# Attention output built transposed, with normalised probabilities, in a two-layer decoder trunk

## The chip, the cores and the metric

One core of a Trainium2 chip, which has eight in two dies. The metric is the device time of one execution in microseconds (us), given as the median of several runs. Everything is float32.

## What is computed

Two layers of a hybrid decoder trunk over 512 tokens of width 1024. Each layer normalises, projects, runs attention (8 query heads that share 2 key heads, 3 branches) beside a gated convolution, projects out, and then runs a channel mixer: dense in the first layer, the two best of 8 experts in the second.

```python
h = rms_norm(x, norm1[layer])
proj = h @ w_in[layer]          # q, 3 x (k, v), gates, conv B, C, h
...
s = einsum(q, k) * scale + rel_bias      # per branch, causal
p = masked_softmax(s, mask)              # exp(s - max) / sum
o = gc[..., 0:1] * o_cmp + gc[..., 1:2] * o_slc + gc[..., 2:3] * o_win
...
mixed = concatenate([rms_norm(o_attn, attn_out_norm[layer]),
                     rms_norm(o_conv, conv_out_norm[layer])], axis=-1)
x = x + mixed @ w_out[layer]
h = rms_norm(x, norm2[layer])
x = x + swiglu(h, ...)          # or moe_swiglu in the second layer
```

With 512 tokens the best 16 of 8 blocks are all blocks and the window covers everything, so the selected and the sliding branch (b = 0 and 1) are both plain causal attention with their own keys and values. The compressed branch attends to 31 blocks.

## The kernel before

The kernel is written in Bass: each engine has its own program, in an order written out by hand, and waits on semaphores. TensorE (pe), VectorE (dve), ScalarE (se), GpSimd (pool) and the DMA queue (sp) run beside each other. Both layers call the same function `layer(L)`.

A layer has these parts. The norm and its turns to hT. The projections of q (four tiles of 128 tokens), k and v, compressed k and v and gates (`natural`, `channels`, L795 and L801), with the turns of queries and keys (L817, L824). The compression (L868, L876). Then the attention loop, of NP + 2 = 34 steps. At its end the sums of the convolution's squares (L985) and the projection out (L1007), whose results VectorE adds to x.

**The attention loop.** Step p has query tile t = p // 8, q = p % 8, the branch b = p % 2 and one pair of heads; a unit u is one head of it (two in a step), over n = 128 (t + 1) keys. For each unit:

- `scores` (L898, TensorE): 64 rows of qT against 64 rows of kT, n columns, into bank u % 2. The two heads of a step lie in the two halves of the rows.
- `scores` (L1199, VectorE): adds the bias from T, negates, keeps the row's extreme. Writes sb_s.
- `probs` (L1421, ScalarE): exponential into sb_p, with the row's sum in `den`.
- `turn` (L911, TensorE): t + 1 transposes of 128 x 128 into bank 2, one step later.
- `pt_copy` (L1207 on VectorE for even units, L1429 on ScalarE for odd ones): bank 2 to sb_pt.
- `values` (L920, TensorE): t + 1 products, turned probabilities stationary (128 columns), values moving (64 columns), into columns of bank 4 (b = 0) or 5 (b = 1).

Between these TensorE's `fill` (L855) gives out products of the convolution's projections, one of 8 for each third of a channel tile, with 512 columns in bank 3. `STEP_FILL` says how many go into each of the three places of a step. When a third is full, ScalarE copies it (`conv_c`, L1386) or VectorE reads it (`conv_z`, L1135, or `conv_b`, L1148); the next third waits for that. `conv_taps` (L1142 to L1144) and `conv_sum` (L1158) are VectorE's too.

Once in a tile come the compressed branch: `cmp_scores` (L932; VectorE L1216 to L1219), `cmp_probs` (L1438), `cmp_turn` (L939), `cmp_values` (L945, into bank 7); and then `coefs` (L1230 to L1232: one over the sums, times the gates), `combine` (L1245 to L1250: the three banks, each times its coefficient, added up in `on`), `attn_norm` (L1448: the sum of squares), `gain` (L1254), `o_turn` (L951: four transposes to bank 7) and `o_copy` (L1452) to mixT, which the projection out reads. For the last tile the turn stands between the projection's first and second token tile.

The functions that the change touches, and the loops that call them:

## Time and profile before

| | us |
|---|---|
| median of 3 runs | 2334.39 (2327.37 to 2335.43) |
| profiled execution | 2332.5 |
| its span in the profile | 2330.7 |
| TensorE busy | 2216.8 (95%) |
| VectorE busy | 397.0 (17%) |
| ScalarE busy | 277.4 (12%) |

The profile is of one execution. Products in float32 leave two records each, transposes one. A record's own duration is longer than its share of the engine, since records overlap in the pipeline; the distance from one start to the next tells what a piece costs. The timeline merges neighbouring records of one line into a piece. Most of the 2330 us are products of the feed-forward and of the experts; the two attention loops take about 170 us each.

### The profile page before, as it was taken

How to read it: one execution, taken by the hardware profiler on the slowest of the kernel's cores; microseconds unless marked ns; L12 is line 12 of the kernel's file. 1: busy time of each engine (PE TensorE's matmuls, PEld its weight loads, DVE VectorE, ACT ScalarE, POOL GpSimd, SP SyncE). 2: the span in 40 equal slices, each digit the busy share in tenths (PEclk: the TensorE clock that was granted, in tenths of full speed). 3: DMA queues.
4: the chain of work that ended last, by engine and by line, in shares of the span. 5: the costliest groups of instructions: out<-in, count | busy, mean ns of one | idle time of the engine just before them, and what ended most of it. 6: DMA issues, size and time to landing. Idle time of an engine off the chain costs nothing.

```text
span 2330.7 us, 29764 instructions
## 1 busy us (share of the span) xinstructions
PE 2216.8 (95%) x12796; PEld 1665.9 (71%) x12796; DVE 397.0 (17%) x1080; ACT 277.4 (12%) x752; POOL 70.3 (3%) x79
## 2 busy tenths in 40 slices
PE   7999998999999989999966999999999999999994
PEld 3556644444444445566556999999999999999994
DVE  2235422000000022254231001010000101010102
ACT  1133311000000012233100000000000000000000
POOL 1100000000000011000000000000000000000001
PEclk9999998999999989999967999999999999999997
DMA  8101106222210402000018556767777777878743
GB/s 322 56 37 37 37 9 266 77 72 72 83 62 0 200 9 72 37 37 1 1 50 356 218 221 244 282 257 287 272 281 276 277 290 283 308 289 304 289 181 118
DMA packets 43987, 382.83 MB, mean 164 GB/s; under 512 B 5362, under 2 KB 5394, under 8 KB 14544
## 3 DMA queue, kind: packets, MB, share of 16 engines
q1 hardware_dynamic: 36208, 355.68, 41.0%
q0 software_dynamic: 4768, 14.92, 2.0%
q10 hardware_dynamic: 2880, 10.32, 1.1%
q8 instruction: 102, 1.67, 0.3%
q14 instruction: 29, 0.24, 0.0%
HBM read 368.46 MB, written 14.54 MB: 164 GB/s over the span
## 4 chain that ended last, share of the span: by engine, by line
PE 93%; DVE 3%; DMA 1%; issue 1%; ACT 1%; POOL 1%; POOLq 0%; DVEq 0%; ACTq 0%
PE ps L382 29%; PE ps L391 14%; PE ps L1022 13%; PE ps L855 7%; PE ps L1031 6%; PE ps L795 6%; PE ps L1007 5%; PE ps L920 2%; PE ps L911 2%; PE ps L898 2%; PE ps L801 1%; PE ps L868 1%; DVE work L1079 1%; PE ps L363 1%; PE ps L339 1%
## 5 line engine op out<-in xcount | busy, mean ns | idle before, releaser
L382 PE MATMUL ps<-work,arena 128*128 128x136 f32 (+3 forms) x5632 | 704.8, 284 | 0.7 <-issue 0.7
L382 PEld LDWEIGHTS ps<-work,arena 128*128 128x128 f32 x5632 | 686.9, 192 | 1.2 <-issue 0.8
L391 PE MATMUL ps<-hid,arena 128*128 128x136 f32 (+3 forms) x2816 | 364.7, 283 | 0.0
L391 PEld LDWEIGHTS ps<-hid,arena 128*128 128x128 f32 x2816 | 348.4, 191 | 0.1
L1022 PE MATMUL ps<-hT,arena 128*128 128x512 f32 x704 | 304.6, 596 | 0.8 <-issue 0.8
L1022 PEld LDWEIGHTS ps<-hT,arena 128*128 128x128 f32 x704 | 134.8, 192 | 170.1 <-issue 170.1
L552 DVE TENSOR_TENSOR hid<-sg,ps 128x136 f32<-128x136 f32 (+3 forms) x176 | 52.8, 300 | 900.2 <-ACT sg L653 899.6
L855 PE MATMUL ps<-hT,arena 128*128 128x512 f32 x384 | 197.6, 617 | 2.0 <-ACT gc L1386 2.0
L653 ACT ACTIVATE sg<-ps 128x136 f32<-128x136 f32 (+3 forms) x176 | 50.5, 287 | 928.4 <-PE ps L382 928.4
L1031 PE MATMUL ps<-arena 128*128 128x512 f32 x352 | 151.3, 593 | 0.8 <-DVE arena L1310 0.8
L795 PE MATMUL ps<-arena,hT 128*128 128x512 f32 (+1 forms) x384 | 131.9, 503 | 0.0
L920 PEld LDWEIGHTS ps<-arena,work 128*128 128x128 f32 x640 | 90.7, 193 | 52.4 <-issue 52.4
L1031 PEld LDWEIGHTS ps<-arena 128*128 128x128 f32 x352 | 67.0, 190 | 85.2 <-issue 83.5
L1007 PE MATMUL ps<-arena 128*128 128x512 f32 x256 | 110.8, 594 | 1.5 <-ACT arena L1452 1.5
L795 PEld LDWEIGHTS ps<-arena,hT 128*128 128x128 f32 x384 | 67.3, 207 | 59.0 <-issue 59.0
L855 PEld LDWEIGHTS ps<-hT,arena 128*128 128x128 f32 x384 | 63.5, 197 | 41.6 <-issue 37.4
L1007 PEld LDWEIGHTS ps<-arena 128*128 128x128 f32 x256 | 48.4, 190 | 61.1 <-issue 61.1
L1421 ACT ACTIVATE work<-work,st 128x128 f32<-128x128 f32 (+3 forms) x128 | 71.8, 561 | 160.3 <-PE ps L911 107.8
L920 PE MATMUL ps<-arena,work 128*128 128x64 f32 x640 | 85.7, 266 | 0.0
L1199 DVE CUSTOM_DVE_ANT_0 work<-ps,arena 128x128 f32<-128x128 f32 (+3 forms) x128 | 57.9, 488 | 111.4 <-PE ps L898 103.5
L1515 POOL TENSOR_TENSOR st<-st,cst 128x1 f32<-128x1 f32 (+3 forms) x38 | 40.5, 1066 | 1125.8 <-DVE st L1058 1125.7
L911 PEld LDWEIGHTS ps<-cst,work 128*128 128x128 f32 x320 | 38.5, 149 | 42.1 <-issue 28.4
(201 smaller groups left out, 991.1 us busy)
## 6 DMA issues: line engine op xcount, KB each, us to landing
arena<-m_w SPq DMA_DIRECT2D x176, 1536.0 KB, 6.6
arena<-f_gu SPq DMA_DIRECT2D x22, 1024.0 KB, 5.0
arena<-w_cv SPq DMA_DIRECT2D x8, 1536.0 KB, 21.6
arena<-f_dn SPq DMA_DIRECT2D x11, 1024.0 KB, 4.8
arena<-w_o SPq DMA_DIRECT2D x4, 2048.0 KB, 7.5
arena<-w_q SPq DMA_DIRECT2D x2, 2048.0 KB, 12.0
arena<-w_kv SPq DMA_DIRECT2D x2, 2048.0 KB, 16.3
arena<-bias_by_query_and_key SPq DMA_DIRECT2D x2, 2048.0 KB, 8.8
```

The source lines that it names most:

```text
L382: m = mm(ps[:, s % 2, j * CAP:j * CAP + W], w[:, k, :], xT[:, k, 0:W], start=(k == 0), stop=(k == KD - 1))
L391: m = mm(ps[:, 2 + j // 2, (j % 2) * CAP:(j % 2) * CAP + W], down_w[s % NSLOT][:, j * P:(j + 1) * P], hid[:, s % 2, 0:W], start=(s == 0 an ...
L552: v.tensor_tensor(hid[:, s % 2, 0:W], sg[:, s % 2, 0:W], ps[:, s % 2, CAP:CAP + W], ALU.mult).then_inc(hid_done, 1)
L795: m = mm(ps[:, bank, col:col + n], hT[:, k, t * P:(t + 1) * P], w[:, k, :], start=(k == 0), stop=(k == KD - 1))
L855: m = mm(ps[:, 3, :], cv_w[CO[i]][:, k, j * P:(j + 1) * P], hT[:, k, :], start=(k == 0), stop=(k == KD - 1))
L911: m = tr(ps[:, 2, i * P:(i + 1) * P], sb_p[:, u % 2, i * P:(i + 1) * P], ident)
L920: m = mm(ps[:, 4 + b, h * DH:(h + 1) * DH], sb_pt[:, u % 2, i * P:(i + 1) * P], V[:, i, b * P + (h // R) * DH:b * P + (h // R + 1) * DH], ...
L1007: m = mm(ps[:, b0 + j, :], mixT[:, 4 * part + k, t * P:(t + 1) * P], WO[part][:, k, hf * 512:(hf + 1) * 512], start=(k == 0), stop=(k == 3))
L1022: m = mm(ps[:, 2 * (i % 2) + j, :], w[:, k, :], hT[:, k, :], start=(k == 0), stop=(k == KD - 1))
L1031: m = mm(ps[:, 2 * t + hf, :], down_w[s][:, i * 512 + t * P:i * 512 + (t + 1) * P], slot[s][:, i * D + hf * 512:i * D + (hf + 1) * 512], s ...
L1199: v.tensor_tensor_reduce(sb_s[:, u % 2, 0:n], ps[:, u % 2, 0:n], T[:, h, 384 - P * t:384 - P * t + n], -1.0, 3e38, ALU.add, ALU.min, negm[ ...
L1421: act(sb_p[:, u % 2, 0:n], sb_s[:, u % 2, 0:n], ACT.Exp, bias=negm[:, u % 16:u % 16 + 1], scale=-1.0, accum_out=den[t % 2][:, 1 + b, h:h + ...
```

## The change

The output of the attention is built with channels on partitions.

- `values`: the values are stationary (64 columns) and the turned probabilities move (128 columns). Key group 0 writes partitions 0 to 63, group 1 partitions 64 to 127 of one bank, 4 + t % 2, into which all three branches of a tile add up. Heads are paired across the groups (r and r + 4), so each step has one head of each group. A step's values run two steps after its scores, in one piece; sb_pt has a second pair of buffers.
- `scale` (new, VectorE): as the sum over branches is now made in the bank, each probability is multiplied by its gate over its sum ahead of the turn, in place. `turn` waits for `scaled`, not for `p_done`. For the compressed branch `cmp_scale` does that.
- `cmp_values`: eight products with 64 stationary columns, added into the tile's bank, in step q = 0 of the next tile.
- `coefs`, `combine`, `gain`, `attn_norm`, `o_turn` and `o_copy` go. New are `o_squares` (ScalarE, from the bank), `evacuate` (VectorE, bank times gain to mixT), `o_reduce` (VectorE, sum over the four column groups) and `o_total` (TensorE, sum over partitions, one column). The sums of the convolution's squares (`conv_totals`) and of the last tile move between the products of the projection's first token tile; one reciprocal root serves all eight sums.
- Keys are no longer doubled for two row halves: kT has 2 groups instead of 4, and the key turns, the key gains and the compressed keys are half as many.
- `STEP_FILL` has the same number of products in another order; `cmp_scores` moves from q = 5 to q = 4.
- Weights for q and w_out are laid out by head pairs on the host.

The diff, cut to its core:

```diff
-STEP_FILL = ((1, 1, 1), (1, 1, 1), (1, 1, 0)) + 2 * ((0, 1, 1), (1, 1, 1), (1, 1, 1)) + (
-    (0, 1, 3), (1, 1, 1), (0, 1, 0), (0, 1, 1), (1, 1, 1), (1, 1, 1), (0, 1, 1), (0, 1, 1), (0, 1, 3),
-    (0, 1, 1), (1, 1, 1), (1, 1, 1), (0, 1, 1), (1, 1, 1), (1, 1, 1), (0, 1, 1), (0, 1, 3), (1, 0, 1),
-    (0, 1, 1), (1, 1, 1), (1, 1, 1))
+STEP_FILL = ((1, 1, 1), (1, 1, 1), (1, 1, 0)) + 9 * ((0, 1, 1), (1, 1, 1), (1, 1, 1))
...
-        sb_s, sb_p, sb_pt = w2[:, 0], w2[:, 1], w2[:, 2]
+        sb_s, sb_p = w2[:, 0], w2[:, 1]
+        sb_pt = [w2[:, 2], arena[:, A_KC + 2 * S:A_KC + 4 * S].rearrange("p (b n) -> p b n", b=2)]
...
+                def scores(p):
+                    t, r, b = p // 8, (p % 8) // 2, p % 2
+                    n = P * (t + 1)
+                    if p == 0:
+                        pe.wait_ge(z_done, 2 * L + 2)
+                    else:
+                        pe.wait_ge(sb_done, NU * L + 2 * p)
...
+                        mm(ps[:, g, 0:n], qT[g * DH:(g + 1) * DH, r, t * P:(t + 1) * P], kT[g * DH:(g + 1) * DH, b, 0:n],
+                           start=True, stop=True).then_inc(s_ps, 1)
...
-                    pe.wait_ge(p_done, NU * L + u + 1)
+                    pe.wait_ge(scaled, NU * L + u + 1)
...
-                def values(u):
-                    t, h, b = unit(u)
-                    pe.wait_ge(pta if u % 2 else ptd, NP * L + u // 2 + 1)
-                    if u % 16 == 0 and t:
-                        pe.wait_ge(o_read, TT * L + t)
+                def values(p):
+                    t, r, b = p // 8, (p % 8) // 2, p % 2
+                    pe.wait_ge(ptd, NP * L + p + 1)
+                    pe.wait_ge(pta, NP * L + p + 1)
+                    if p % 8 == 0 and t >= 2:
+                        pe.wait_ge(mix_done, TT * L + t - 1)
+                        pe.wait_ge(osq_done, TT * L + t - 1)
                     for i in range(t + 1):
-                        m = mm(ps[:, 4 + b, h * DH:(h + 1) * DH], sb_pt[:, u % 2, i * P:(i + 1) * P],
-                               V[:, i, b * P + (h // R) * DH:b * P + (h // R + 1) * DH], start=(i == 0), stop=(i == t))
+                        for g in range(G):
+                            m = mm(ps[g * DH:(g + 1) * DH, 4 + t % 2, r * P:(r + 1) * P], V[:, i, b * P + g * DH:b * P + (g + 1) * DH],
+                                   sb_pt[p % 2][:, g, i * P:(i + 1) * P], start=(p % 8 == 0 and i == 0), stop=(b == 1 and i == t and r == R - 1),
+                                   skip_group_check=True)
...
                 def cmp_values(t):
                     pe.wait_ge(cpt_done, TT * L + t + 1)
-                    for g in range(G):
-                        m = mm(ps[:, 7, g * 256:(g + 1) * 256], PcT[:, g, :], vbd[:, g, :], start=True, stop=True)
+                    for r in range(R):
+                        for g in range(G):
+                            m = mm(ps[g * DH:(g + 1) * DH, 4 + t % 2, r * P:(r + 1) * P], vbd[:, g, r * DH:(r + 1) * DH], PcT[:, g, :],
+                                   start=False, stop=False, skip_group_check=True)
                     m.then_inc(co_ps, 1)
 
-                def o_turn(t):
-                    pe.wait_ge(og_done, TT * L + t + 1)
-                    for i in range(4):
-                        m = tr(ps[:, 7, i * P:(i + 1) * P], on[:, i * P:(i + 1) * P], ident)
-                    m.then_inc(ot_ps, 1)
+                def o_total(t):
+                    pe.wait_ge(osum_done, TT * L + t + 1)
+                    mm(ps[:, 7, 448 + t:449 + t], o_sum, ones[:, 0:1], start=True, stop=True).then_inc(sums_ps, 1)
+
+                def conv_totals():
+                    pe.wait_ge(sqs_done, CT * (L + 1))
+                    for t in range(TT):
+                        m = mm(ps[:, 7, 452 + t:453 + t], sqsum[:, t * P:(t + 1) * P], ones[:, 0:1], start=True, stop=True)
+                    m.then_inc(sums_ps, 1)
...
                     if 1 <= p <= NP:
                         turn(2 * p - 2)
                     fill(f[1])
                     if p >= 2:
-                        values(2 * p - 3)
+                        values(p - 2)
+                    if q == 0 and t:
+                        cmp_values(t - 1)
                     if 1 <= p <= NP:
                         turn(2 * p - 1)
                     fill(f[2])
-                    if 1 <= p <= NP:
-                        values(2 * p - 2)
                     if p == 3:
                         cmp_keys()
-                    if q == 4 and t:
-                        o_turn(t - 1)
-                    if q == 5:
+                    if q == 3 and t:
+                        o_total(t - 1)
+                    if q == 4:
                         cmp_scores(t)
                     if q == 6:
                         cmp_turn(t)
-                    if q == 7:
-                        cmp_values(t)
-
-                pe.wait_ge(sqs_done, CT * (L + 1))
-                pe.wait_ge(cpt_done, TT * (L + 1))
-                for t in range(TT):
-                    m = mm(ps[:, 6, t:t + 1], sqsum[:, t * P:(t + 1) * P], ones[:, 0:1], start=True, stop=True)
...
+                        if t == 0 and j == 1:
+                            o_total(TT - 1)
+                            conv_totals()
...
+                def scale(p):
+                    t, r, b = p // 8, (p % 8) // 2, p % 2
+                    n = P * (t + 1)
+                    d = den[:, (2 * p) % 16:(2 * p) % 16 + 2]
+                    dve.wait_ge(p_done, NU * L + 2 * p + 2)
+                    after(v.reciprocal(d, d))
+                    if p == 0:
+                        dve.wait_ge(gate_done, L + 1)
+                    for g in range(G):
+                        v.tensor_scalar(sb_p[:, g, 0:n], sb_p[:, g, 0:n], d[:, g:g + 1], gts[:, t, R * g + r, 1 + b:2 + b],
+                                        ALU.mult, ALU.mult).then_inc(scaled, 1)
+
...
+                def cmp_scale(t):
                     n = KD * t + 7
                     dve.wait_ge(cp_done, TT * L + t + 1)
-                    after(v.tensor_reduce(den[t % 2][:, 0, :], Pc[:, :, 0:n], AX, ALU.add))
-
-                def coefs(t):
-                    dve.wait_ge(p_done, NU * L + 16 * t + 16)
-                    dve.wait_ge(gate_done, L + 1)
-                    dflat = st[:, 40 + 64 * (t % 2):64 + 64 * (t % 2)]
-                    after(v.tensor_scalar(dflat, dflat, 1e-30, None, ALU.max))
-                    after(v.reciprocal(dflat, dflat))
-                    after(v.tensor_tensor(coef, den[t % 2], gts[:, t, :, :].rearrange("p h b -> p b h"), ALU.mult))
+                    after(v.tensor_reduce(denc, Pc[:, :, 0:n], AX, ALU.add))
+                    after(v.tensor_scalar(denc, denc, 1e-30, None, ALU.max))
+                    after(v.reciprocal(denc, denc))
+                    after(v.tensor_tensor(coefc, denc, gts[:, t, :, 0], ALU.mult))
                     if t == 0:
-                        after(v.tensor_scalar(coef[:, 0, :], coef[:, 0, :], cst[:, C_VALID:C_VALID + 1], None, ALU.mult))
-
-                def combine(t):
-                    o3 = on[:, :].rearrange("p (h n) -> p h n", h=H)
-                    t3 = on_t[:, :].rearrange("p (h n) -> p h n", h=H)
-                    bank = lambda b: ps[:, b, :].rearrange("p (h n) -> p h n", h=H)
-                    dve.wait_ge(co_ps, TT * L + t + 1)
-                    if TT * L + t:
-                        dve.wait_ge(ot_ps, TT * L + t)
-                    dve.wait_ge(kct_ps, L + 1)
-                    dve.wait_ge(o_ps, NU * L + 16 * t + 16)
-                    after(v.tensor_tensor(o3, bank(4), bc_last(coef[:, 1, :], DH), ALU.mult))
-                    v.tensor_tensor(t3, bank(5), bc_last(coef[:, 2, :], DH), ALU.mult).then_inc(o_read, 1)
-                    dve.wait_ge(o_read, TT * L + t + 1)
-                    after(v.tensor_tensor(o3, o3, t3, ALU.add))
-                    after(v.tensor_tensor(t3, bank(7), bc_last(coef[:, 0, :], DH), ALU.mult))
-                    v.tensor_tensor(o3, o3, t3, ALU.add).then_inc(comb_done, 1)
-
-                def gain(t):
-                    dve.wait_ge(ssa_done, TT * L + t + 1)
-                    v.tensor_tensor(on[:, :], on[:, :], pb[:, B_AN:B_QN], ALU.mult).then_inc(og_done, 1)
+                        after(v.tensor_scalar(coefc, coefc, cst[:, C_VALID:C_VALID + 1], None, ALU.mult))
+                    v.tensor_tensor(Pc[:, :, 0:n], Pc[:, :, 0:n], bc_last(coefc, n), ALU.mult).then_inc(cps_done, 1)
+
+                def evacuate(t):
+                    dve.wait_ge(osq_done, TT * L + t + 1)
+                    v.tensor_tensor(mixT[:, 0:R, t * P:(t + 1) * P], ps[:, 4 + t % 2, :].rearrange("p (r n) -> p r n", r=R),
+                                    bc_last(pc[:, PC_AN:PC_AN + R], P), ALU.mult).then_inc(mix_done, 1)
+
+                def o_reduce(t):
+                    dve.wait_ge(osq_done, TT * L + t + 1)
+                    if t:
+                        dve.wait_ge(sums_ps, (TT + 1) * L + t)
+                    v.tensor_reduce(o_sum, o_sq.rearrange("p (r n) -> p n r", r=R), AX, ALU.add).then_inc(osum_done, 1)
...
                         pt_copy(2 * p - 2)
+                    if p < NP:
+                        scale(p)
                     if p == 0:
                         cmp_keys()
                     if p == 1:
                         cmp_vals()
-                    if q == 0 and t:
-                        coefs(t - 1)
                     if q == 1 and t:
-                        combine(t - 1)
-                    if q == 3 and t:
-                        gain(t - 1)
+                        evacuate(t - 1)
+                    if q == 2 and t:
+                        o_reduce(t - 1)
+                    if q == 4:
+                        cmp_scores(t)
...
+                def o_squares(t):
+                    se.wait_ge(o_ps, NP * L + 8 * t + 8)
+                    se.wait_ge(co_ps, TT * L + t + 1)
+                    if t:
+                        se.wait_ge(osum_done, TT * L + t)
+                    act(o_sq, ps[:, 4 + t % 2, :], ACT.Square).then_inc(osq_done, 1)
...
-                    if q == 2 and t:
-                        attn_norm(t - 1)
                     if p == 3:
                         cmp_keys()
-                    if q == 4 and t:
-                        o_copy(t - 1)
-                    if q == 5:
+                    if q == 1 and t:
+                        o_squares(t - 1)
+                    if q == 4:
                         cmp_probs(t)
                     if q == 6:
                         cmp_pt(t)
...
```

## Rows read from the trace of the kernel before

**Rows 1.** Busy time in the second layer's attention stage: span, then PE, PEld, DVE, ACT, POOL.

```profile
955.00:1122.00 167.00, 162.06 (x887) 102.36 (x885) 80.65 (x245) 65.66 (x191) 0.69 (x1) 1.00 0.04 13
```

**Rows 2.** Waits of TensorE in the second layer's attention stage: total us, times, longest us.

```profile
PE ps L911 <- DVE work L1207: 3.0, 3, 1.7
PE ps L855 <- ACT gc L1386: 1.0, 1, 1.0
```

**Rows 3.** TensorE's timeline, steps 28 and 29: start us, us, engine line op tiles xrecords.

```profile
1091.13 1.00 PE L920 MATMUL ps<-arena,work 128*128 128x64 f32 x8
1092.06 1.13 PE L898 MATMUL ps<-arena 64*128 64x512 f32 x4
1093.12 1.13 PE L855 MATMUL ps<-hT,arena 128*128 128x512 f32 x2
1094.08 0.60 PE L911 MATMUL ps<-cst,work 128*128 128x128 f32 x4
1094.52 1.02 PE L855 MATMUL ps<-hT,arena 128*128 128x512 f32 x2
1095.38 1.00 PE L920 MATMUL ps<-arena,work 128*128 128x64 f32 x8
1096.22 0.60 PE L911 MATMUL ps<-cst,work 128*128 128x128 f32 x4
...
1098.36 0.61 PE L951 MATMUL ps<-cst,qk 128*128 128x128 f32 x4
1098.90 1.13 PE L898 MATMUL ps<-arena 64*128 64x512 f32 x4
```

**Rows 4.** TensorE's timeline, compression output and first scores, second layer.

```profile
955.51 0.63 PE L876 MATMUL ps<-pc,hidc 128*31 128x64 f32 x8
956.08 0.49 PE L898 MATMUL ps<-arena 64*128 64x128 f32 x4
```

**Rows 5.** TensorE's timeline, end of the loop and projection, second layer.

```profile
1106.20 1.11 PE L898 MATMUL ps<-arena 64*128 64x512 f32 x4
...
1110.45 0.63 PE L911 MATMUL ps<-cst,work 128*128 128x128 f32 x4 [1.72 <-DVE work L1207]
...
1121.34 1.00 PE L985 MATMUL ps<-cst,arena 128*128 128x1 f32 x8
1122.20 13.98 PE L1007 MATMUL ps<-arena 128*128 128x512 f32 x32
1136.02 0.60 PE L951 MATMUL ps<-cst,qk 128*128 128x128 f32 x4
1137.39 1.96 PE L1007 MATMUL ps<-arena 128*128 128x512 f32 x4 [0.77 <-ACT arena L1452]
```

**Rows 6.** Timelines of VectorE and TensorE at the last two key tiles, second layer.

```profile
930.67 0.76 DVE L1122 TENSOR_TENSOR qk<-work,pb 128x256 f32<-128x256 f32 x2
...
931.49 1.12 PE L824 MATMUL ps<-cst,qk 128*128 128x128 f32 x4 [1.37 <-DVE qk L1122]
```

**Rows 7.** Groups of VectorE, second layer's stage: shapes xcount, busy us, mean ns, idle.

```profile
L1199 DVE CUSTOM_DVE_ANT_0 work<-ps,arena 128x512 f32<-128x512 f32 x16 | 10.4, 688 | 18.6 <-PE ps L898 15.8 <-issue 2.7
...
L1199 DVE CUSTOM_DVE_ANT_0 work<-ps,arena 128x256 f32<-128x256 f32 x16 | 6.1, 422 | 12.4 <-PE ps L898 12.3
L1207 DVE COPY work<-ps 128x512 f32<-128x512 f32 x8 | 5.5, 689 | 2.9 <-PE ps L911 2.8
...
L1144 DVE SCALAR_TENSOR_TENSOR arena<-zc,pc,arena 128x512 f32<-128x512 f32 x4 | 3.0, 752 | 0.1
...
L1142 DVE TENSOR_SCALAR arena<-zc,pc 128x512 f32<-128x512 f32 x4 | 1.9, 481 | 0.0
...
L1231 DVE RECIPROCAL st<-st 128x24 f32<-128x24 f32 x4 | 1.2, 303 | 0.1
```

**Rows 8.** Groups of ScalarE, second layer's stage.

```profile
L1421 ACT ACTIVATE work<-work,st 128x512 f32<-128x512 f32 x16 | 11.5, 722 | 26.2 <-PE ps L911 19.0 <-DVE st L1199 7.2
...
L1429 ACT COPY work<-ps 128x512 f32<-128x512 f32 x8 | 4.5, 566 | 2.4 <-PE ps L911 2.4
```

More of the change, by code:

```diff
@@ L89 @@
 A_WC = 2 * SLOT
-assert A_END <= ARENA and 2 * LP * HID <= KD * 512 and CO[2:] == (0, 1) and KCW * KD >= 2 * S
+assert A_END <= ARENA and 2 * LP * HID <= KD * 512 and CO[2:] == (0, 1) and KCW * KD >= 4 * S
 C_ID, C_ONE, C_TRI, C_IOTA = 0, P, 2 * P, 3 * P
@@ L190, in build @@
         rh = st[:, 16:24]
-        ssa = st[:, 24:28]
-        ra = st[:, 28:32]
-        rc = st[:, 32:36]
+        rac = st[:, 24:32]
         posb = st[:, 36:38]
-        den = [st[:, 40 + 64 * i:64 + 64 * i].rearrange("p (b h) -> p b h", b=3) for i in range(2)]
-        coef = st[:, 64:88].rearrange("p (b h) -> p b h", b=3)
+        den = st[:, 40:56]
+        denc = st[:, 56:64]
+        coefc = st[:, 64:72]
         negm = st[:, 88:104]
@@ L822, in kt @@
                     pe.wait_ge(v_done, TT * L + t + 1)
-                    for i in range(4):
+                    for i in range(2):
                         m = tr(ps[:, 4 + t, i * P:(i + 1) * P], kn[:, i * P:(i + 1) * P], ident)
@@ L957, in layer @@
                     if p < NP:
-                        scores(2 * p)
-                        scores(2 * p + 1)
+                        scores(p)
                     fill(f[0])
@@ L1365, in kt @@
                     se.wait_ge(kt_ps, TT * L + t + 1)
-                    nc.scalar.copy(kT[:, :, t * P:(t + 1) * P], ps[:, 4 + t, :].rearrange("p (k n) -> p k n", k=4)).then_inc(kt_done, 1)
+                    nc.scalar.copy(kT[:, :, t * P:(t + 1) * P], ps[:, 4 + t, 0:2 * P].rearrange("p (k n) -> p k n", k=2)).then_inc(kt_done, 1)
                 for a in range(2):
@@ L1407, in cmp_keys @@
                     se.wait_ge(kct_ps, L + 1)
[L1408 removed]
+                    nc.scalar.copy(kcT[:, 0:NCMP], ps[:, 7, 256:256 + NCMP]).then_inc(kct_done, 1)
                 def probs(u):
[L1411 to L1413 removed]
+                    n = P * (u // 16 + 1)
                     se.wait_ge(sb_done, NU * L + u + 1)
```

164 lines of the change are left out of this document (65 added, 99 removed).

## The prediction

> **What bounds the kernel now.** I read the busy time of the attention stage of the second layer first, then who waits for whom, then the order of TensorE's pieces. In that stage of 167 us TensorE is busy for 162, at its full clock; VectorE is busy for 81 and ScalarE for 66 [rows 1]. The list of waits says the same: about 5 us in which TensorE stands still, of which 3.0 are for VectorE's copy of turned probabilities and 1.0 for a ScalarE copy of a convolution third [rows 2]. So an edit is worth what it takes from TensorE's own pieces, until VectorE or ScalarE comes late. The first layer repeats the stage, so what follows is worked out for one layer and doubled. I name a head pair with one branch a step (32 of them, 8 for each query tile t = 0 to 3), and T1 the moment at which TensorE begins the second turn of a step.
>
> **Values on TensorE.** Pieces are told by the distance of their starts. A values group of 8 records (4 key tiles) takes 0.84 us, a turn of four tiles 0.44, a fill product of 512 columns 0.86 [rows 3]: 0.11 us for each record with 128 stationary columns, however few move, which is the weight load, and 0.43 for each with 512 moving columns. After the change a values record has 64 stationary columns and 128 moving ones, and the moving side then sets 0.107 to 0.111 (the turns move 128 columns in that). That the load of half the columns is below this is bounded by L876: its 8 records of 31 columns with 64 moving take 0.57 from start to next start [rows 4]. So the stream is no shorter for one product; it is halved only if the two column halves run side by side. No row shows column halves. Row halves are the nearest: the two score products of 512 columns take 1.06 together, where one full product takes 0.86 [rows 3]. I take side by side.
>
> Such a group has a price of its own, and the scores show it. Before them the values piece is 0.93 instead of 0.84; they take 1.06 where their columns explain 0.85; the fill product behind them takes 0.96 instead of 0.86 [rows 3]. That is 0.40 for going into another split of the array and back. With a load half as long on the way in I take 0.35 (ends: 0, if columns switch freely, and 0.40). A step's values cost 0.22 x 2(t+1) - 0.11 now and 0.22(t+1) + 0.35 then. The difference is +0.23, +0.01, -0.21 and -0.43 us for t = 0 to 3, eight times each: **-3.2 us** in a layer.
>
> On the page TensorEngine Tiling the Trainium skill says (Key Properties) that a change of tiling mode drains TensorE; this trace agrees for row halves, by the 0.40. The same section says that different tiles can load and multiply in parallel; whether that holds for column halves no row here shows. By the first rule alone this term would be +14.6 us in a layer (8 x 0.22 x 10 more), by both it is the -3.2.
>
> **Other work taken from TensorE or given to it.** The output turn goes (0.54 each, three in the loop), and a one-column sum comes for each tile (two records, 0.22): **-1.0**. Compressed values change from 4 records of 256 columns to 8 pairs of 128 and stay at about 0.9, without a switch of their own, since they stand behind values. At the end the convolution sums (0.86) leave the gap ahead of the projection, and the last output turn with its wait (1137.39 - 1136.02 = 1.37) leaves its middle, where ten one-column records (1.08) come in [rows 5]: **-1.15**. The squares, the output's copy and the reduction that these need take 0.6 + 0.7 + 0.7 behind the last values and are hidden by the 6.9 us of the first eight projection products. The key turns are two instead of four, and one VectorE multiply of some 0.4 goes from the chain that ends the 1.37 us wait for the last key tile [rows 6]: **-1.3**, between -0.9 (the turns alone) and -1.8.
>
> **The wait that is added.** Now a turn starts when ScalarE's exponential is ready. Then VectorE must first take both exponentials of the step, a reciprocal of two columns and two multiplies in place. No row shows these; the nearest are L1231 (0.30 for 24 columns) for the first, taken at 0.17 and 0.035 to the next instruction (0.1 to 0.3), and L1142 (0.48 for 512 columns, a new one after 0.41) for each multiply (0.41 to 0.75, the latter with L1144 as the price of its second scalar) [rows 7]. By these prices, shortened for fewer columns, 64 multiplies and 32 reciprocals are some 28 us more VectorE work in a layer; the combination with its gain and coefficients takes about 18 away, evacuation, sums and compressed scaling bring 9. Worse is the order. VectorE now stands blocked in each step until the second exponential is done, and everything that is queued behind it comes later: convolution z, b, taps and sums, compressed scores, and the next step's score reads, for which TensorE's next turn waits.
>
> For t = 3: the second exponential starts at T1 + 0.76 (end of the turn) and takes 0.72 and 0.09 more for its accumulator [rows 8], so VectorE starts at T1 + 1.62, its first scaled half is there at 2.34 and it is free at 2.64. TensorE needs that half at T1 + 0.54 + 0.86 + 0.09 + 1.06 = 2.56 in steps without a first fill, so the plain step just fits, at 5.0 or 5.9 us. But anything of length E that VectorE does then delays its score reads and its copy by E, against a slack of 0.4 us where the next step has no first fill and 1.3 where it has one; and the next convolution third, at T1 + 3.05, waits for z or b, at T1 + 3.37. With z and b at 0.69 (as L1207), taps at 0.48 + 0.75 + 0.75 plus gaps = 2.05 [rows 7] this gives, step by step: t = 3, z with the sum of squares 0.95, taps 0.7. For t = 2 (rows between those shown): z with evacuation 1.1, taps with the sum 1.2, b behind compressed scores 0.9. For t = 1, with 0.42 for a score read [rows 7]: z 0.55, taps with evacuation 1.35, b 0.55, the other three 0.7. For t = 0: 1.2 for compressed keys, b and compressed scaling. In all **+9.3 us** (4 if the slack is twice what I take, 14 at the dearer multiply). Against that the waits of before in these steps go, 1.0 for the ScalarE copy (compressed probabilities no longer stand in front of it), 0.6 for exponentials and 0.6 of VectorE's 3.0 [rows 2]: **-2.2**.
>
> **The last four steps**, which have no fill, are now a chain: turn, exponential, reciprocal, two multiplies, two score reads, copy, turn. Followed from the start of step 30, with VectorE late by compressed scaling (five small passes, put at 0.2 to 0.4 each by L1231 and L1199's short form, 1.5) and b (0.7): the turn of u59 comes at 5.2, step 31 at 6.1, the turn of u60 at 7.5, of u61 at 9.75, of u62 at 12.05, of u63 at 14.55; ScalarE's copy of that (0.57, behind 0.72) ends at 15.9, the last values at 16.9. Before, it was 1122.20 - 1106.20 = 16.0, with a wait of 1.72 in it [rows 5]. The 1.0 more comes on top of 0.86 and of 3 x 0.43 that I credited above: **+3.1**.
>
> **Sum**: -3.2 - 1.0 - 1.15 - 1.3 + 9.3 - 2.2 + 3.1 = +3.55 us in a layer, +7.1 in both. Projection, feed-forward and experts are untouched. The profiled execution took 2332.5 us (span 2330.7), which gives 2339.6; the median of the three runs lies 1.9 above it, so the forecast is **2341.5 us**. The core's own range is 2331 to 2352.
>
> **Rivals.** *The halves run one after the other* (ends slower). Then values cost 0.22(t+1) more in each step, 8 x 0.22 x 10 = 17.8 us in a layer, of which some 4 come back since VectorE's chain gains that time: +17 in a layer, 2368. It decides if a pair of values records takes 0.21 instead of 0.11. For it: no row shows such a pair. Against: row halves do run together. *VectorE's queue stays hidden.* If the steps' slack takes in z, b and taps, the 9.3 go and the last steps remain: -5.75 in a layer, 2323; and a little below if the last steps are shorter. For it: VectorE is idle for half the stage [rows 1]. Against: it is idle in waits, with its work behind them. *The multiplies cost more than L1142*, by their second scalar or since they write what they read: at 0.75 instead of 0.48 for 512 columns the plain step of t = 3 no longer fits by 0.1 to 0.6 us and each listed wait grows: +5 to +8 in a layer more, 2355. *The change isn't what it says*: should the turns still find a scaled half late by a fixed wait, it is the same case.
>
> **How the numbers follow.** Chances: forecast 0.50, halves in turn 0.15, queue hidden 0.20, dearer multiplies 0.15. A measurement of this kernel can tell about 0.5% (11.7 us) from no change: 2322.7 to 2346.1. Faster by more: half of the hidden case and little else, 0.13. Slower by more: the serial and the dear case and a quarter of the forecast's own range, 0.40. The rest, 0.47, is within. The range reaches from 2319 to 2368: it leaves out some of the hidden case and the upper half of the serial one.
>
> **What would show it.** In the profile after: values records in pairs, a group for t = 3 some 1.1 us to the next turn and 0.5 for t = 0 (2.0 would be the serial case); the piece ahead of it lengthened by 0.1; the in-place multiplies at 0.48 us for 512 columns and some 0.3 for 128; TensorE's waits in the stage from 5 us to some 15, on VectorE's scaling, copies and z; VectorE busy for about 100 us of it. The weakest step is the sum of the waits, the next is that column halves pair as row halves do.

## The result, and the profile after

The changed kernel takes 2343.91 us (median of 8 runs, 2340.35 to 2346.39) beside 2331.78 for the kernel before (8 runs, 2327.37 to 2335.86): ratio 1.0048, 95% interval 1.0036 to 1.0059. It is slower by 12.1 us, where 7.1 was forecast. The forecast time of 2341.5 came closer than this, 2.4 us away, because it was counted from the median of three runs of the kernel before, 2334.4, which lies 2.6 above the median of eight; that part of the closeness is luck. The profiled execution took 2343.9, its span 2342.0, against 2332.5 and 2330.7.

The page of the kernel after, span and busy time by engine:

```profile
span 2342.0 us, 30066 instructions
PE 2207.9 (94%) x12858; PEld 1616.3 (69%) x12858; DVE 432.5 (18%) x1236; ACT 270.4 (12%) x736; POOL 69.7 (3%) x77
```

TensorE has 8.9 us less to do than before (2216.8) and the kernel takes 11.3 us more of span: work was traded for waiting. The same second-layer stage as in [rows 1], span, then PE, PEld, DVE, ACT, POOL, and its granted TensorE clock (1.00 is 2.4 GHz, 0.50 is 1.2):

```profile
959.00:1134.00 175.00, 158.00 (x921) 78.18 (x919) 102.35 (x331) 63.70 (x185) 0.69 (x1) 0.98 0.04 13
```

The stage is 175 us instead of 167, TensorE is busy for 158 of it instead of 162, and VectorE for 102 instead of 81. TensorE's waits there, to be set against the 5 us of [rows 2] (total us, times, longest):

```profile
PE ps L906 <- DVE arena L1212: 5.9, 6, 2.6
PE ps L906 <- DVE work L1212: 3.5, 3, 1.8
PE ps L855 <- DVE zc L1130: 2.7, 3, 1.2
PE ps L906 <- DVE work L1204: 2.5, 2, 1.7
PE ps L855 <- DVE arena L1143: 1.7, 3, 0.8
PE ps L918 <- ACT arena L1416: 0.8, 1, 0.8
```

17.1 us. L906 is the turn, L1212 VectorE's copy of turned probabilities, L1204 the new multiply, L855 the fill product, L1130 and L1143 the reads of the convolution's z and b. Only 2.5 us are waits for the multiply itself. The others are for work that VectorE used to have done long before. Why it is late stands in VectorE's groups by shape (shapes, count | busy us, mean ns | idle before, and what ended it):

```profile
L1204 DVE TENSOR_SCALAR work<-work,st,gts 128x512 f32<-128x512 f32 x16 | 8.0, 543 | 0.3
L1204 DVE TENSOR_SCALAR work<-work,st,gts 128x384 f32<-128x384 f32 x16 | 7.0, 477 | 0.3
L1204 DVE TENSOR_SCALAR work<-work,st,gts 128x256 f32<-128x256 f32 x16 | 5.9, 409 | 0.3
L1200 DVE RECIPROCAL st<-st 128x2 f32<-128x2 f32 x32 | 5.3, 166 | 60.2 <-ACT work L1408 60.2
L1204 DVE TENSOR_SCALAR work<-work,st,gts 128x128 f32<-128x128 f32 x16 | 4.8, 344 | 0.3
L1247 DVE TENSOR_REDUCE qk<-qk 128x128 f32<-128x512 f32 x3 | 3.1, 1030 | 0.0
```

The reciprocal's line is the case in one row: VectorE stands for 60.2 us of the stage at the reciprocal, for ScalarE's exponential (L1408), with everything else queued behind it.

The timeline of TensorE in steps 28, 29 (as [rows 3]) and from step 30 to the projection (as [rows 5]):

```profile
1092.41 1.02 PE L855 MATMUL ps<-hT,arena 128*128 128x512 f32 x2
1093.36 1.09 PE L918 MATMUL ps<-work,arena 128*64 128x128 f32 x16
1094.38 0.66 PE L906 MATMUL ps<-cst,work 128*128 128x128 f32 x4
1094.88 1.02 PE L855 MATMUL ps<-hT,arena 128*128 128x512 f32 x2
...
1107.72 0.63 PE L906 MATMUL ps<-cst,work 128*128 128x128 f32 x4 [0.80 <-DVE arena L1212]
...
1115.92 1.13 PE L893 MATMUL ps<-arena 64*128 64x512 f32 x4
...
1121.26 1.09 PE L906 MATMUL ps<-cst,work 128*128 128x128 f32 x4 [2.60 <-DVE arena L1212]
1122.14 0.63 PE L938 MATMUL ps<-cst,Pc 128*128 128x128 f32 x2
1122.71 2.04 PE L893 MATMUL ps<-arena 64*128 64x512 f32 x4
...
1126.84 0.63 PE L906 MATMUL ps<-cst,work 128*128 128x128 f32 x4 [0.48 <-DVE work L1212]
1129.21 0.66 PE L906 MATMUL ps<-cst,work 128*128 128x128 f32 x4 [1.75 <-DVE work L1204]
...
1133.12 1.09 PE L918 MATMUL ps<-arena 128*64 128x128 f32 x16 [0.77 <-ACT arena L1416]
1134.14 2.41 PE L1001 MATMUL ps<-arena 128*128 128x512 f32 x5
```

A values group (L918) of eight pairs of records takes 1.02 us to the next start (1093.36 to 1094.38), the fill product ahead of it 0.95 instead of 0.86 and the turn behind it 0.50 instead of 0.44. Behind the wait of 2.60 the score products take 1.97 us (1122.71 to 1124.68) where two steps earlier they take 1.06 (1115.92 to 1116.98): there TensorE has fallen to half its clock. What it does just before the fall is to stand in that wait.

### The profile page after: what moved, and what is told of

Its sections match the earlier page's. It is cut to its first block, busy times and chain, and to the rows that moved or that the text cites. A ratio compares the mean times of both kernels' runs of the same rounds, so it can differ in the third digit from the quotient of the medians.

```text
span 2342.0 us, 30066 instructions
## 1 busy us (share of the span) xinstructions
PE 2207.9 (94%) x12858; PEld 1616.3 (69%) x12858; DVE 432.5 (18%) x1236; ACT 270.4 (12%) x736; POOL 69.7 (3%) x77
## 4 chain that ended last, share of the span: by engine, by line
PE 90%; DVE 5%; issue 2%; DMA 1%; ACT 1%; POOL 1%; POOLq 0%; DVEq 0%; ACTq 0%
PE ps L382 29%; PE ps L391 14%; PE ps L1019 13%; PE ps L1028 6%; PE ps L855 6%; PE ps L795 6%; PE ps L1001 5%; PE ps L906 2%; PE ps L918 2%; PE ps L893 1%; PE ps L801 1%; PE ps L868 1%; DVE work L1076 1%; DVE work L1204 1%; PE ps L363 1%
## 5 line engine op out<-in xcount | busy, mean ns | idle before, releaser
L1019 PE MATMUL ps<-hT,arena 128*128 128x512 f32 x704 | 304.7, 596 | 0.8 <-issue 0.8
L855 PE MATMUL ps<-hT,arena 128*128 128x512 f32 x384 | 203.6, 629 | 8.6 <-DVE zc L1130 5.3
L855 PEld LDWEIGHTS ps<-hT,arena 128*128 128x128 f32 x384 | 63.4, 198 | 51.2 <-issue 37.6
L1408 ACT ACTIVATE work<-work,st 128x128 f32<-128x128 f32 (+3 forms) x128 | 71.8, 561 | 191.9 <-PE ps L906 110.1
L906 PEld LDWEIGHTS ps<-cst,work 128*128 128x128 f32 x320 | 37.7, 144 | 67.5 <-issue 46.3
L906 PE MATMUL ps<-cst,work 128*128 128x128 f32 x320 | 62.2, 294 | 23.4 <-DVE arena L1212 11.8
L1497 POOL TENSOR_TENSOR st<-st,cst 128x8 f32<-128x8 f32 (+2 forms) x36 | 39.8, 1107 | 1138.0 <-DVE st L1055 1138.0
L1301 DVE TENSOR_TENSOR arena<-work,ps 128x512 f32<-128x512 f32 x22 | 15.2, 689 | 289.3 <-PE ps L1019 289.3
```

Source lines behind the costliest of these rows:

```text
L855: m = mm(ps[:, 3, :], cv_w[CO[i]][:, k, j * P:(j + 1) * P], hT[:, k, :], start=(k == 0), stop=(k == KD - 1))
L906: m = tr(ps[:, 2, i * P:(i + 1) * P], sb_p[:, u % 2, i * P:(i + 1) * P], ident)
L1019: m = mm(ps[:, 2 * (i % 2) + j, :], w[:, k, :], hT[:, k, :], start=(k == 0), stop=(k == KD - 1))
L1408: act(sb_p[:, u % 2, 0:n], sb_s[:, u % 2, 0:n], ACT.Exp, bias=negm[:, u % 16:u % 16 + 1], scale=-1.0, accum_out=den[:, u % 16:u % 16 + 1]) ...
```

## The experiments

All times are medians beside the kernel before on the same chip, which ran at 2332 to 2334 us throughout. Edits are against the changed kernel, unless something else is said.

### Is it the multiply, or where it waits? The scaling taken out

```diff
-                    pe.wait_ge(scaled, NU * L + u + 1)
+                    pe.wait_ge(p_done, NU * L + u + 1)
...
-                    if p < NP:
-                        scale(p)
```

> The changed kernel without its in-place scaling of the two full branches: reciprocal and multiplies are left out (so these two branches are neither normalised nor gated), and a turn waits for the exponential alone, as in the kernel before. Theory (VectorE's queue stands blocked behind the exponentials, and TensorE waits for it): of some 17 us of TensorE's waits in a loop about 13 go, and with them the two stretches at half clock; 15 us in a layer, 2313 us. Rival (the column halves and their switches are dearer than thought, the waits are a minor part): no more than 5 us in a layer, 2334 us.

Measured: 2312.89 us, ratio 0.9919 (0.9898 to 0.994). That is 31 us below the changed kernel; TensorE's waits fall from 33.8 us in both loops to 13.2.

The same work was then left in VectorE's program at the same place and with the same instructions, but on columns that nobody needs, with nothing waited for (the turn waits for the exponential alone, as above):

```diff
-                    d = den[:, (2 * p) % 16:(2 * p) % 16 + 2]
-                    dve.wait_ge(p_done, NU * L + 2 * p + 2)
+                    d = st[:, 200:202]
...
-                        v.tensor_scalar(sb_p[:, g, 0:n], sb_p[:, g, 0:n], d[:, g:g + 1], ...
+                        v.tensor_scalar(spare_p[:, g, 0:n], spare_p[:, g, 0:n], d[:, g:g + 1], ...
```

> The same reciprocals and multiplies in the same places of VectorE's order and of the same sizes, but on spare columns, so that they wait for no exponential and no turn waits for them (the two full branches are neither normalised nor gated). Theory (the wait and the order behind it): nearly as short as without scaling, 2313 to 2322 us. Rival (VectorE has too much work, 102 us instead of 81 in a loop): as the changed kernel, 2338 to 2344 us.

Measured: 2312.28 us, 0.9909 (0.9888 to 0.993), and waits of 14.0 us. The multiplies and reciprocals, 31 us of VectorE in a layer (8.0 + 7.0 + 5.9 + 4.8 + 5.3), cost nothing at all; the 31 us of both layers are the price of the waits around them, VectorE's for the exponentials and the turn's for the scaled probabilities. It also gives a size for what the change takes from TensorE: with these waits away it is some 20 us shorter than the kernel before, though such a kernel neither normalises nor gates.

### Do column halves run side by side?

Both key groups were written to the same column half, so that two products of a pair can't run together:

```diff
-                            m = mm(ps[g * DH:(g + 1) * DH, 4 + t % 2, r * P:(r + 1) * P], ...
+                            m = mm(ps[0:DH, 4 + t % 2, r * P:(r + 1) * P], ...
```

> All products of values and of compressed values write partitions 0 to 63 (the second group's output goes on top of the first's, so the attention output is wrong): both products of a pair are in the same column half. Theory (halves run side by side in the changed kernel): a values group of t = 3 goes from 1.02 to some 1.87 us, 16 to 18 us in a layer less some 4 of waits, 2368 to 2378 us. Rival (the halves ran in turn anyway): 2344 us.

Measured: 2373.89 us (one run), 30 above the changed kernel. The values group of that kernel:

```profile
1117.64 1.96 PE L918 MATMUL ps<-work,arena 128*64 128x128 f32 x16
1119.53 0.66 PE L906 MATMUL ps<-cst,work 128*128 128x128 f32 x4
```

1.89 us for the same sixteen records against 1.02. Over a layer that is 0.87/4 x 8 x 10 = 17.4, and 3.7 more for the compressed values (1.84 instead of some 0.9, four times); twice that is 42, of which 6.9 come back since the waits fall from 33.8 to 26.9. The 5 us that are left may be the clock, with 6.8 us at half clock in the loops of this profile against 20.5. Side by side is what the changed kernel has.

### Is it VectorE's order? The work of once a tile ahead of the scaling

Evacuation, compressed keys and convolution taps now stand in front of `scale(p)` in VectorE's step, where it has nothing to do but wait; the evacuation moves to q = 2 and compressed keys and values one step on:

```diff
                         pt_copy(2 * p - 2)
-                    if p < NP:
-                        scale(p)
-                    if p == 0:
-                        cmp_keys()
                     if p == 1:
+                        cmp_keys()
+                    if p == 2:
                         cmp_vals()
...
                         conv_taps(i)
+                    if p < NP:
+                        scale(p)
+                    if p == NP + 1:
+                        evacuate(TT - 1)
+                    if q == 4:
+                        cmp_scores(t)
```

> Only VectorE's order is changed: convolution taps and sums, the compressed scaling, evacuation (one step later) and reduction stand ahead of the step's scaling, in the time in which VectorE waited for the exponentials; compressed keys and values one step later. Nothing is left out. Theory: of the waits on copies (1.24, 0.36, 0.44, 1.31, 0.38, 1.76, 0.80 and 2.60 in the second layer) about 6 us go in a layer, those on z and b (4.3) stay; 2330 to 2334 us. Rival (total of VectorE's work decides): 2342 to 2346 us.

Measured: 2322.81 us, 0.995 (0.9933 to 0.9967). Of the 31 us that the waits cost, 21 are the order of the queue behind them, much more than I expected. Its waits in the second layer's stage:

```profile
PE ps L906 <- DVE work L1204: 3.5, 4, 1.7
PE ps L855 <- DVE arena L1143: 1.7, 3, 0.8
PE ps L906 <- DVE arena L1212: 1.2, 1, 1.2
PE ps L855 <- DVE zc L1130: 1.1, 3, 0.5
PE ps L918 <- ACT arena L1417: 0.8, 1, 0.8
PE ps L906 <- DVE work L1212: 0.7, 1, 0.7
```

The waits for copies went from 9.4 to 1.9 and those for z from 2.7 to 1.1; the one for the multiply itself, 3.5, is now the largest.

### Can the convolution's thirds wait instead?

```diff
-STEP_FILL = ((1, 1, 1), (1, 1, 1), (1, 1, 0)) + 9 * ((0, 1, 1), (1, 1, 1), (1, 1, 1))
+STEP_FILL = ((1, 1, 1), (1, 1, 1), (1, 1, 0)) + 9 * ((0, 0, 2), (1, 1, 1), (1, 1, 1))
```

> The changed kernel with (0, 0, 2) instead of (0, 1, 1) in the nine steps that begin a convolution third: the third's first product stands behind the second turn instead of ahead of the values. Theory: TensorE's waits on z and b (0.52, 0.46, 0.34, 0.97, 0.79, 1.23: 4.3 us in the second layer) go, but the values and the second turn come 0.86 earlier and meet VectorE's copy, which gives a part of it back in the steps behind evacuation or taps; 2336 to 2341 us. Rival (the wait only moves to the copy): 2343 to 2346 us.

Measured: 2350.27 us, 1.0069 (1.0046 to 1.0093). The expectation was wrong in sign, with four runs from 2343.6 to 2352.8. The waits for z and b are gone, as meant, and the waits for copies take their place and more:

```profile
PE ps L906 <- DVE arena L1212: 7.9, 7, 2.6
PE ps L906 <- DVE work L1212: 7.3, 6, 2.1
PE ps L906 <- DVE work L1204: 2.5, 2, 1.7
PE ps L918 <- ACT arena L1416: 0.8, 1, 0.8
```

The product that was taken from between the turn and the values had been the cover of VectorE's late copy. With VectorE as late as here, holding a product back didn't mend the wait: it moved it to the next place where the two meet.

### What the fill order is worth

In the kernel before, with the changed kernel's `STEP_FILL` and nothing else:

> The kernel before with nothing changed but the order of the convolution's products among the steps, which is that of the changed kernel. The new order has no part in the loss if this is as before, 2330 to 2335 us; if it has one, the thirds that end in steps with compressed work meet ScalarE and VectorE there and cost up to 5 us in a layer, 2342 us. The theory says the first, with at most 2 us in a layer.

Measured: 2341.47 us, 1.0034 (1.0022 to 1.0045), some 8 us where at most 4 were expected. Its waits in the second layer:

```profile
PE ps L908 <- DVE work L1204: 3.6, 3, 1.7
PE ps L917 <- DVE qk L1243: 1.4, 3, 0.5
PE ps L852 <- ACT gc L1383: 1.0, 1, 1.0
PE ps L852 <- DVE zc L1132: 0.5, 1, 0.5
```

L917 is that kernel's values and L1243 its read of a bank in `combine`. The old order gave three products to the place behind the second turn in steps 9, 17 and 25, where `combine` stands. These waits explain 5 of the 8 us (15.8 in both loops, 10.8 before). Its profile also has 13.7 us of its loops at half clock against 6.8, which by the sizes found below is 1.5 to 3 us more. What is left I can't name by a row.

And the other way round, the changed kernel with the old order:

> The change with the fill order of the kernel before, and nothing else altered. In the kernel before, the changed kernel's fill order alone cost 7 to 9 us, because it takes away the three products that stand beside VectorE's combine. Here combine is gone. Theory A (the old order was fitted to combine, so it is worth nothing without it): within 3 us of the changed kernel, 2341 to 2347, or slower, up to 2350, because it holds three products back for places where nothing waits. Theory B (the old order is better whatever VectorE does): 2334 to 2339, the whole difference to the kernel before given back.

Measured: 2343.1 us, 1.0047 (1.003 to 1.0064), as the changed kernel itself. Theory A holds: an order fitted to `combine` is worth 8 us with it and nothing without it. So the new order isn't a part of the loss.

### What the clock costs: products in the longest wait

Two more products of 512 columns in each layer, whose result nobody reads, where TensorE waits 2.60 us:

```diff
+                    if p == NP - 2:
+                        pe.wait_ge(cv_done, CT * (L + 1))
+                        for k in range(2):
+                            mm(ps[:, 3, :], hT[:, k, 0:P], hT[:, k, :], start=True, stop=True)
```

> The changed kernel with two more products of 512 columns (results unused, 1.7 us of work) in step 30 of each layer, in the 2.6 us in which TensorE waits for a copy. Theory (the wait lowers the granted clock, and the pieces behind it then run at 1.2 GHz): no stretch at half clock behind step 30 and 1 to 3 us in a layer less in spite of the added work; 2338 to 2342 us. Rival (the clock falls for another reason): the fall stays, 2344 us or a little above.

Measured: 2342.71 us, 1.0043 (1.0026 to 1.006), with more work in it no slower than the changed kernel; the 1.2 us between them are within the noise. The same 8 us of both kernels, the clock is the figure ahead of the last two (the changed kernel first, then this one):

```profile
1117.00:1125.00 8.00, 5.40 (x35) 3.23 (x34) 5.37 (x16) 3.37 (x8) 0.00 (x0) 0.79 0.00 1
```

```profile
1117.00:1125.00 8.00, 6.40 (x50) 3.54 (x46) 6.14 (x18) 4.32 (x10) 0.00 (x0) 1.00 0.00 1
```

In this profile the fall behind this wait is gone in both layers; one early in each loop is left. This makes it likely that the wait brings the fall and doesn't show it, since a wait of the same length can stay without one. Here are such a wait in the first layer of the changed kernel with the old fill order, and the 8 us around it, with the clock at 1.00:

```profile
295.18 0.63 PE L909 MATMUL ps<-cst,work 128*128 128x128 f32 x4 [2.60 <-DVE arena L1215]
```

```profile
291.00:299.00 8.00, 4.93 (x50) 3.38 (x50) 6.11 (x18) 3.91 (x9) 0.00 (x0) 1.00 0.66 258
```

In three profiles with this wait (changed, old fill order, thirds later), each with two layers, four of the six waits have a fall beside their end and two have none. With the two products in it the time from the values of step 28 to the last values is 14.73 us instead of 15.55, so the fall there costs 0.8 us net, although the pieces in it are 1.6 longer: a part of it runs down waits that come anyway.

### Versions that use this

As the extras-first kernel, but with the fills spread over more steps, so that the last four have some:

```diff
+STEP_FILL = ((1, 1, 1), (1, 1, 1), (1, 1, 0)) + 7 * ((0, 0, 2), (1, 1, 1), (1, 1, 1)) + 2 * ((0, 0, 2), (0, 1, 1), (0, 1, 1), (0, 1, 1))
```

> The run with VectorE's extras ahead of the scaling, and with that the products of the convolution spread over all 32 steps ((0, 0, 2) to begin a third, and two groups of four steps at the end), so that the last two steps have products too. Theory: the waits on z and b go in part and the chain of the last steps is covered by four products: 4 to 7 us in a layer below the 2322.8 of that run, 2309 to 2316 us. Rival (the copy waits take their place): 2320 to 2325 us.

Measured: 2318.72 us, 0.9947 (0.9931 to 0.9964), between the theory and the rival; the (0, 0, 2) brings back waits for copies, 7.4 us in a layer. Without it:

```diff
+STEP_FILL = ((1, 1, 1), (1, 1, 1), (1, 1, 0)) + 7 * ((0, 1, 1), (1, 1, 1), (1, 1, 1)) + 8 * ((0, 1, 1),)
```

> VectorE's work once a tile ahead of the scaling, as in e3, and the fills spread over 32 steps instead of 30, so that the last four steps of the loop have a product between each wait and the next. e3 had 3.7 us of waits in its last four steps (1.75, 0.77, 0.69, 0.47). Theory (the end of the loop is what is left): half of it goes in each layer, 2319 to 2322. Rival (what is taken from the steps ahead makes them late in turn, as the other spread did in part): 2323 to 2328.

Measured: 2312.86 us, 0.9909 (0.9892 to 0.9927), 10 us below the extras-first kernel and more than either theory gave. Its last steps on TensorE:

```profile
1096.42 1.02 PE L855 MATMUL ps<-hT,arena 128*128 128x512 f32 x2
1098.33 0.66 PE L906 MATMUL ps<-cst,work 128*128 128x128 f32 x4 [0.89 <-DVE work L1204]
1098.91 1.09 PE L918 MATMUL ps<-work,arena 128*64 128x128 f32 x16
```

One wait of 0.89 for the last multiply and one of 0.31 ahead of it, where there were 1.18, 0.47, 0.69 and 1.75 (the 0.77 before the last values is in both), and no fall of the clock in either loop.

Then the pair's wait taken apart, each head for itself:

```diff
-                    dve.wait_ge(p_done, NU * L + 2 * p + 2)
-                    after(v.reciprocal(d, d))
                     for g in range(G):
+                        dve.wait_ge(p_done, NU * L + 2 * p + g + 1)
+                        after(v.reciprocal(d[:, g:g + 1], d[:, g:g + 1]))
```

> As e9, but VectorE waits for each head's exponential on its own: one over the sum and the multiply of the first head run while ScalarE still makes the second head's probabilities. It adds 32 short instructions and takes the pair's wait away. Theory (the wait for the scaled probabilities is the time from the second exponential to the end of the multiplies, of which one multiply of 0.54 us goes): the eight waits of 7.0 us in e3 fall to 3 or less in a layer, 2312 to 2318. Rival (the queue of VectorE behind it is what makes the wait, not the multiplies): within 2 us of e9.

Measured: 2313.32 us, 0.9915 (0.9899 to 0.9932). The waits fall by 2.5 us (12.0 to 9.5), the time not: the rival holds, and 32 more reciprocals in a layer are no gain.

One run went astray:

> The kernel before with its last fills spread as in e9: in each of its last seven steps with a first fill that one goes, and the products stand in steps 30 and 31 instead; the three products beside combine stay. It tells what part of e9's 20 us is due to the spread and not to the change. Theory (the last four steps of the kernel before wait only 1.72 and 0.76 us, so the spread is worth at most 2.5 us in a layer there): 2327 to 2331. Rival (the spread is worth as much here as between e3 and e9, 10 us): 2321 to 2325, and half of e9's gain would be had without the change.

Measured: 2334.22 us, 1.0006 (0.9993 to 1.0018). The kernel that ran under this name was the kernel before without the edit, so it tells nothing of either theory, and what the spread alone would bring to the kernel before stays open. It does give the kernel before against itself: within 0.2%, and with the clock at half for 10.2 us of its attention loops in this profile against 6.8 us in the first one, two of the three falls at other places. Where a fall lies is therefore not a property of a kernel alone.

## Why the prediction came out as it did

The table puts the runs together: median, TensorE's waits for other engines in both attention loops by the list of waits, and the time in these loops at half clock, summed over the trace's stretches. Waits and clock are of the one profiled run of each kernel.

| kernel | us | waits | half clock |
|---|---|---|---|
| before | 2331.8 | 10.8 | 6.8 |
| before, changed kernel's fill order | 2341.5 | 15.8 | 13.7 |
| changed | 2343.9 | 33.8 | 20.5 |
| changed, old fill order | 2343.1 | 32.4 | 23.9 |
| two products in the wait | 2342.7 | 31.8 | 6.8 |
| thirds later | 2350.3 | 39.1 | 30.7 |
| extras first | 2322.8 | 18.0 | 6.8 |
| extras first, fills over 32 steps | 2312.9 | 12.0 | 0 |
| no scaling | 2312.9 | 13.2 | 0 |
| scaling off the path | 2312.3 | 14.0 | 0 |

From the changed kernel to the best one the time falls by 31.0 and the waits by 21.8. The other 9.2 go with 20.5 us of half clock, 0.45 us for each; between other pairs of rows it is 0.1 to 0.6, so this is a size and no law. The executions of one kernel among themselves give a second size. The 41 of the kernel before that ran beside the experiments took from 2327.4 us, at a granted clock of 0.969 over the whole span (144 us at half clock), to 2336.5, at 0.962 (177 us): 0.2 to 0.3 us for each us of half clock. So the 9 us between the fastest and the slowest execution of one kernel go with the clock, and a part of a difference between two medians can do so too. With 10.3 to 13.7 us more of half clock in the changed kernel's loops (20.5 less 10.2 or 6.8) the 12.1 us come apart like this: waits +23.0, clock +2 to +6, and work that TensorE no longer has -13 to -17, as what is left.

- **Direction, mechanism and place were right.** VectorE's queue, blocked for 60 us in a layer, and not its amount of work: [rows 1] showed 81 us of work in 167, and the run with that work off the path shows that 31 more us fit in for nothing.
- **The sum of the waits** (the step called weakest): the loop ahead of its last four steps has 11.4 us against the 9.3 of the prediction (its own list adds up to 9.2). By tile it is 3.4 for 1.2 (t = 0), 2.5 for 3.15, 3.5 for 3.2 and 2.0 for 1.65. So the step that failed in size is t = 0: there I named the compressed keys, b and the compressed scaling and gave them 1.2 in all. The keys alone brought 1.24, as VectorE also waits 0.80 for GpSimd in them, behind a blocked scaling; the eight copies of the compressed values (L1179, 1.80 us in a row), which I hadn't named, stand ahead of 0.36 more; the multiply itself was late by 0.80, b by 0.52, and 0.44 follow the compressed scaling.
- **The last four steps**: 18.2 us from the scores of step 30 to the projection (1115.92 to 1134.14), 16.9 forecast, 16.0 before. The waits came nearly as followed (the turn of u59 at 5.3 for 5.2). Of the missing 1.3 the fall of the clock behind the 2.60 is 0.8, by the run with products in that wait, which takes 17.4; the other 0.5 is there too and builds up along the chain (0.2, 0.3, 0.4 and 0.4 at the turns of u60 to u63), which was priced a little short in each link, the multiply with it.
- **The clock had no term.** [rows 1] shows 1.00 for the stage and I carried it over, though the forecast itself put a wait of some 2.5 us where there had been 1.72 [rows 5]. This is the one step that is missing and not only mis-sized.
- **Values on TensorE** were better than forecast: a group of t = 3 costs 1.02 + 0.09 + 0.06 = 1.17 with what it adds to its neighbours, 1.23 forecast, against 1.68 before. Going into column halves and back costs 0.31, 0.35 forecast. That column halves pair was the second weakest step; 1.89 against 1.02 shows it. The Trainium skill's page TensorEngine Tiling (Key Properties) has different tiles load and multiply in parallel; the trace agrees for column halves, by these two figures. Two slips of the working: by its own formula the difference is +0.24, +0.02, -0.20 and -0.42, which makes -2.9 and not -3.2 in a layer; and the rival of halves in turn has +17 in a layer beside 2368, where 17.6 less 4 gives +13.6 and 2369. The run with the halves in turn took 2374.
- **The multiply**: 0.543 us for 512 columns, 0.48 forecast, 0.344 for 128; the rival of dear multiplies (0.75) is out. The slope is (543 - 344)/384 = 0.52 ns for a column. On the page VectorE: DVE Perf Modes (Mode 2×_2P) the Trainium skill gives float32 `tensor_scalar` twice the rate of a two-tensor operation; the trace agrees: the two-tensor product of the compressed scaling (L1236) goes by 1.05 ns, 418 ns for 248 columns and 284 for 120. The reduction over four column groups is 1.03 where 0.7 was taken, and hidden where it was said to be.
- **Start of the layer**: the key turns and the shorter chain gave 0.94 us in a layer (from the layer's start to the first scores), at the lower end of 0.9 to 1.8, 1.3 taken.
- **The rival of a hidden queue** (2323) is wrong for this kernel, but its time is nearly that of the extras-first kernel. The slack was there; the order of VectorE's program didn't let the work into it.

In all: 20 us of waits were forecast for both layers with the last steps (10.2 each, the cover lost there included) and 23.0 came, 13.3 us of work were to go and 13 to 17 went, and 2 to 6 us of clock were not seen. The 5 us between +7.1 and +12.1 are made of these; how they divide between waits, work and clock isn't settled more closely than that.

## What to carry to other kernels

When a step that waits for another engine is put into an in-order queue, price what stands behind it, not the step: here 31 us of multiplies and reciprocals in each layer cost nothing, and the waits around them 31 us in both layers together. Work that comes once in a while belongs ahead of such a wait, in the time that is spent waiting anyway; that order and a product between each of the last waits turned +12 us into -20 with the same instructions (what the kernel before would gain by the same spreading of the products wasn't measured). And a hand-made interleaving is fitted to the code around it: the same fill order was worth 8 us beside `combine` and nothing without it, so it is to be measured again with each larger change. Last, where two versions differ by a few us, compare their granted clocks before a cause is named.

## What the runs showed of the hardware

- Float32 products with 64 stationary and 128 moving columns in the two column halves run together: 0.127 us for a pair of records, one in each half (1.02/8), against 0.236 with both in one half (1.89/8), a group's own price of going in included.
- TensorE's clock fell to 1.2 GHz inside a loop whose average busy share is 90%, beside the end of a wait of 2.60 us in four of six cases. With the wait filled by two products that nobody needs it stayed at 2.4 GHz in both layers, and the kernel was no slower for them. In two profiles of the same kernel the falls lay partly at different places, for 6.8 and 10.2 us in all, with spans of 2330.7 and 2330.4. Over 41 executions of it the granted clock went from 0.962 to 0.969 and the time from 2336.5 to 2327.4 us.
- VectorE's work in place with two scalars on 128 x 512 float32 takes 0.543 us; with one scalar, and not in place, it takes 0.481 [rows 7].
